# Banded attention: two units at a time, halves of the partitions interleaved on TensorE

## The reference, cut to what matters

```
logits = einsum('bnqhgd,bnkhd->bnhgqk', qb, kw) * (dh ** -0.5)
logits = where(valid, logits, -inf)          # band of 128 keys; block 0 has no block before it
m = maximum(max(logits, axis=-1), sink)
probs = exp(logits - m[..., None])
denom = sum(probs, axis=-1) + exp(sink - m)
out = einsum('bnhgqk,bnkhd->bnhgqd', probs, vw) / denom[..., None]
```

## Time and profile before

| | us |
|---|---|
| median of 3 runs | 4322.08 |
| lowest, highest | 4319.68, 4322.27 |
| profiled execution, its time | 4317.04 |
| its span | 4315.2 |
| TensorE busy | 4166.0 (97%) |
| VectorE busy | 1942.0 (45%) |
| GpSimd busy | 1112.1 (26%) |
| ScalarE busy | 701.1 (16%) |

### The profile page before, as it was taken

The page is one execution under the profiler, slowest core; times in us unless marked ns, Lnnn a source line. Parts: engine busy times, 40 slices in busy tenths (PEclk is TensorE's granted clock), DMA queues, the critical chain, the costliest instruction groups (busy, mean ns, idle before and its releaser), DMA issues.

```text
span 4315.2 us, 43399 instructions
## 1 busy us (share of the span) xinstructions
PE 4166.0 (97%) x17144; PEld 2943.7 (68%) x17144; DVE 1942.0 (45%) x3582; ACT 701.1 (16%) x1452; POOL 1112.1 (26%) x960
## 2 busy tenths in 40 slices
PE   7999999999999999999999999999999989989998
PEld 3448884445588744788833488888886447838887
DVE  3446663246377622433245443333334754454432
ACT  2321110113311100100014310010001321211000
POOL 0003430002344200344300134434442051003443
PEclk9999999998999999999999999999999899989999
DMA  3114443210154442222210122222222132112222
GB/s 119 49 54 168 173 174 135 93 64 30 40 189 175 152 143 88 72 88 86 95 49 20 40 88 88 83 74 88 88 90 66 59 112 59 36 40 78 88 83 73
DMA packets 128105, 387.61 MB, mean 90 GB/s; under 512 B 37984, under 2 KB 41056, under 8 KB 117152
## 3 DMA queue, kind: packets, MB, share of 16 engines
q1 hardware_dynamic: 112592, 302.56, 21.4%
q10 hardware_dynamic: 13824, 75.50, 4.7%
q0 software_dynamic: 1488, 6.78, 0.4%
HBM read 376.40 MB, written 8.39 MB: 89 GB/s over the span
## 4 chain that ended last, share of the span: by engine, by line
PE 93%; DVE 4%; ACT 2%; issue 1%; DMA 0%; POOL 0%; DVEq 0%; ACTq 0%; POOLq 0%
PE bank L762 92%; DVE temporary L2620 1%; PE bank L1202 1%; DVE normed L1911 1%; ACT normed L1449 0%; PE bank L1109 0%; DMA vector_columns<-in_vectors_dram 0%; ACT temporary L1449 0%; ACT area_b L1449 0%; PE bank L1331 0%; DVE area_a L2433 0%; ACT squares L1449 0%; DVE rstd L1926 0%; ACT L1449 0%; DVE temporary L2144 0%
## 5 line engine op out<-in xcount | busy, mean ns | idle before, releaser
L762 PE MATMUL bank<-normed,weight_ring 128*128 128x256 f32 (+2 forms) x3312 | 1025.7, 464 | 17.6 <-DVE normed L1917 5.8
L762 PEld LDWEIGHTS bank<-normed,weight_ring 128*128 128x128 f32 (+1 forms) x3312 | 635.6, 194 | 367.9 <-issue 285.2
L762 PE MATMUL bank<-area_a,weight_ring 128*128 128x512 f32 (+1 forms) x1776 | 636.5, 515 | 8.2 <-issue 8.2
L762 PE MATMUL bank<-area_b,weight_ring 128*128 128x256 f32 (+3 forms) x2000 | 589.2, 441 | 5.9 <-issue 2.8
L762 PEld LDWEIGHTS bank<-area_a,weight_ring 128*128 128x128 f32 x1776 | 339.7, 192 | 282.1 <-issue 259.9
L695 POOL TENSOR_TENSOR area_d<-weight_ring 128x512 f32<-128x512 f32 (+1 forms) x92 | 114.7, 1246 | 1571.0 <-PE bank L762 816.6
L762 PEld LDWEIGHTS bank<-area_b,weight_ring 128*128 128x128 f32 (+2 forms) x2000 | 375.5, 188 | 186.8 <-issue 145.9
L762 PE MATMUL bank<-area_b 128*128 128x256 f32 (+2 forms) x1584 | 345.0, 378 | 16.2 <-ACT area_d L1449 16.2
L762 PEld LDWEIGHTS bank<-area_b 128*128 128x128 f32 (+1 forms) x1584 | 287.1, 194 | 61.0 <-ACT area_d L1449 16.9
L762 PE MATMUL bank<-area_b,area_d 128*128 128x256 f32 x1440 | 326.1, 379 | 0.0
L762 PEld LDWEIGHTS bank<-area_b,area_d 128*128 128x128 f32 x1440 | 273.8, 190 | 37.5 <-issue 0.2
(11 more groups left out here) (296 smaller groups left out, 4788.7 us busy)
## 6 DMA issues: line engine op xcount, KB each, us to landing
weight_ring<-in_weights_dram SPq DMA_DIRECT2D x429, 512.0 KB, 4.6
area_b<-in_weights_dram ACTq DMA_DIRECT2D x48, 1024.0 KB, 4.9
weight_ring<-in_weights_dram SPq DMA_DIRECT2D x35, 1024.0 KB, 4.9
area_b<-in_weights_dram ACTq DMA_DIRECT2D x48, 512.0 KB, 6.3
weight_ring<-in_weights_dram SPq DMA_DIRECT2D x40, 384.0 KB, 4.4
weight_ring<-in_weights_dram SPq DMA_DIRECT2D x24, 256.0 KB, 3.8
low_scratch<-area_d SPq DMA_DIRECT2D x16, 256.0 KB, 2.0
area_d<-low_scratch SPq DMA_DIRECT2D x16, 256.0 KB, 2.7
```

Of the source, the lines that this page charges most:

```text
L762: i = pe.matmul(out, lhsT, rhs, start=start, stop=stop)
```

## The change

Two units that differ only in the half become a pair w (16 pairs). TensorE issues the scores of a pair in the order head 0 half 0, head 0 half 1, head 1 half 0, head 1 half 1, into two products: scores now use banks 0 to 3, and only turned probabilities and outputs use banks 4 to 7, so all eight banks serve the stage. Outputs of a pair are issued key block by key block with the halves alternating, each matmul over both heads at once (256 columns), so there are half as many. The lag is 3 pairs for transposes and 4 for outputs.

VectorE handles the columns of a pair together: the maximum with the sink, the subtraction, the negation, the sum and the reciprocal run once a pair on four columns. ScalarE takes the exponential of the sink once a pair, ahead of the four exponentials, and puts the copies of the turned probabilities in between them. The results are copied out of the banks by VectorE, not ScalarE, four pairs behind. ScalarE now also waits, before it overwrites a turned buffer, for the outputs that read it.

```diff
 stage("at_in", 12 + 4, 2 * 12, 12 * DB + 2 * DB)
-stage("at", 0, 32 * 3, 0)
+stage("at", 32, 32 * 2, 0)
 stage("at_out", DB, 0, DB * DB)
...
         AT_ORDER = {}
-        LAG = 5
-        for u in range(32 + LAG + 1):
-            for what, v in (("scores", u), ("turned", u - LAG), ("output", u - LAG - 1)):
-                if 0 <= v < 32:
-                    AT_ORDER[what, v] = len(AT_ORDER)
+        LAG = 3
+        for w in range(16 + LAG + 1):
+            for what, q in (("turned", w - LAG), ("output", w - LAG - 1)):
+                if 0 <= q < 16:
+                    for half in range(2):
+                        AT_ORDER[what, 2 * q + half] = len(AT_ORDER)
         def at_probs(v):
             return (TM if v % 8 < 4 else D)[:, v % 4, :]
-        def at_column(what, v):
-            o = 16 * ("max", "sum", "sink", "one").index(what) + 2 * (v % 8)
-            return SM[:, o:o + 2]
+        def at_columns(what, w):
+            o = 16 * ("max", "sum", "sink", "one").index(what) + 4 * (w % 4)
+            return SM[:, o:o + 4]
+        def at_scores(v):
+            return AT["at"][0] + v
...
-                po.wait_ge(S("at_one_over"), v + 1)
+                po.wait_ge(S("at_one_over"), v // 2 + 1)
                 for e in range(2):
                     w = at_probs(v)[:, 256 * e + lo:256 * e + 256]
-                    i = po.tensor_scalar(w, w, at_column("one", v)[:, e:e + 1], None, ALU.mult)
+                    i = po.tensor_scalar(w, w, at_columns("one", v // 2)[:, 2 * (v % 2) + e:2 * (v % 2) + e + 1], None, ALU.mult)
                 i.then_inc(S("at_probs"), 1)
...
-            for u in range(32 + LAG + 1):
-                if u < 32:
-                    n, g, half = u // 8, u // 2 % 4, u % 2
-                    rows = slice(64 * half, 64 * half + 64)
-                    s = small()
+            for w in range(16 + LAG + 1):
+                if w < 16:
+                    n, g = w // 4, w % 4
+                    keys = slice((n - 1) * P, (n + 1) * P) if n else slice(0, P)
+                    ms = [product(), product()]
                     for e in range(2):
-                        keys = slice((n - 1) * P, (n + 1) * P) if n else slice(0, P)
-                        mm(sbank(s)[:, 256 * e + (0 if n else 128):256 * e + 256], A[rows, 2 * g + e, n * P:(n + 1) * P],
-                           A[rows, 8 + g, keys], True, True, small_full if e == 1 else None)
-                if 0 <= u - LAG < 32:
-                    v = u - LAG
-                    s = small()
-                    pe.wait_ge(S("at_probs"), v + 1)
-                    for e in range(2):
-                        for b in range(0 if v >= 8 else 1, 2):
-                            i = pe.transpose(sbank(s)[:, (2 * e + b) * P:(2 * e + b + 1) * P],
-                                             at_probs(v)[:, (2 * e + b) * P:(2 * e + b + 1) * P], const("ident"))
-                    i.then_inc(small_full, 1)
-                if u >= LAG + 1:
-                    v = u - LAG - 1
-                    n, g, half = v // 8, v // 2 % 4, v % 2
-                    s = small()
-                    sdone(pe, at_small("turned", v))
-                    for e in range(2):
-                        for b in range(0 if n else 1, 2):
-                            at_tokens = n - 1 + b
-                            mm(sbank(s)[64 * half:64 * half + 64, e * P:(e + 1) * P],
-                               A[:, 12 + at_tokens // 2, at_tokens % 2 * 256 + 64 * g:at_tokens % 2 * 256 + 64 * g + 64],
-                               B[:, 12 + v % 4, (2 * e + b) * P:(2 * e + b + 1) * P], b == (0 if n else 1), b == 1,
-                               small_full if e == 1 and b == 1 else None)
+                        for half in range(2):
+                            rows = slice(64 * half, 64 * half + 64)
+                            mm(pbank(ms[half])[:, 256 * e + (0 if n else 128):256 * e + 256],
+                               A[rows, 2 * g + e, n * P:(n + 1) * P], A[rows, 8 + g, keys], True, True,
+                               product_full if e == 1 else None)
+                if 0 <= w - LAG < 16:
+                    for v in (2 * (w - LAG), 2 * (w - LAG) + 1):
+                        s = small()
+                        pe.wait_ge(S("at_probs"), v + 1)
+                        for e in range(2):
+                            for b in range(0 if v >= 8 else 1, 2):
+                                i = pe.transpose(sbank(s)[:, (2 * e + b) * P:(2 * e + b + 1) * P],
+                                                 at_probs(v)[:, (2 * e + b) * P:(2 * e + b + 1) * P], const("ident"))
+                        i.then_inc(small_full, 1)
+                if w >= LAG + 1:
+                    q = w - LAG - 1
+                    n, g = q // 4, q % 4
+                    ss = [small(), small()]
+                    sdone(pe, at_small("turned", 2 * q))
+                    sdone(pe, at_small("turned", 2 * q + 1))
+                    for b in range(0 if n else 1, 2):
+                        t = n - 1 + b
+                        values = A[:, 12 + t // 2, t % 2 * 256 + 64 * g:t % 2 * 256 + 64 * g + 64]
+                        for half in range(2):
+                            turned = B[:, 12 + (2 * q + half) % 4, :].rearrange("p (e b t) -> p b e t", b=2, t=P)
+                            out = sbank(ss[half])[64 * half:64 * half + 64, 0:256].rearrange("p (e t) -> p e t", t=P)
+                            mm(out, values, turned[:, b], b == (0 if n else 1), b == 1, small_full if b == 1 else None)
...
-            for u in range(32 + LAG):
-                if u < 32:
-                    act.wait_ge(S("at_minus_max"), u + 1)
-                    n, g, half = u // 8, u // 2 % 4, u % 2
-                    for e in range(2):
-                        p = at_probs(u)[:, 256 * e + (0 if n else 128):256 * e + 256]
-                        a(p, p, ACT.Exp, bias=at_column("max", u)[:, e:e + 1],
-                          accum_out=at_column("sum", u)[:, e:e + 1]).then_inc(S("at_exp"), 1)
-                    a(at_column("sink", u), at_column("sink", u), ACT.Exp).then_inc(S("at_exp"), 1)
-                if 0 <= u - LAG + 1 < 32:
-                    v = u - LAG + 1
-                    s = at_small("turned", v)
-                    sfull(act, s)
-                    out, turned = (x.rearrange("p (e k) -> p e k", e=2)[:, :, 0 if v >= 8 else P:]
-                                   for x in (B[:, 12 + v % 4, :], sbank(s)[:, :]))
-                    stook(a(out, turned, ACT.Identity), s)
-                if u >= LAG:
-                    v = u - LAG
-                    n, g, half = v // 8, v // 2 % 4, v % 2
-                    s = at_small("output", v)
-                    sfull(act, s)
-                    rows = slice(64 * half, 64 * half + 64)
-                    stook(a(B[rows, 4 + 2 * g:6 + 2 * g, n * P:(n + 1) * P],
-                            sbank(s)[rows, 0:256].rearrange("p (e t) -> p e t", e=2), ACT.Identity), s)
+            for w in range(16 + LAG - 1):
+                if w < 16:
+                    act.wait_ge(S("at_minus_max"), w + 1)
+                    a(at_columns("sink", w), at_columns("sink", w), ACT.Exp).then_inc(S("at_exp"), 1)
+                for half in range(2):
+                    if w < 16:
+                        for e in range(2):
+                            o = 2 * half + e
+                            p = at_probs(2 * w + half)[:, 256 * e + (0 if w >= 4 else 128):256 * e + 256]
+                            a(p, p, ACT.Exp, bias=at_columns("max", w)[:, o:o + 1],
+                              accum_out=at_columns("sum", w)[:, o:o + 1]).then_inc(S("at_exp"), 1)
+                    if w >= LAG - 1:
+                        v = 2 * (w - LAG + 1) + half
+                        s = at_small("turned", v)
+                        sfull(act, s)
+                        if v >= 4:
+                            sfull(act, at_small("output", v - 4))
+                        out, turned = (x.rearrange("p (e k) -> p e k", e=2)[:, :, 0 if v >= 8 else P:]
+                                       for x in (B[:, 12 + v % 4, :], sbank(s)[:, :]))
+                        stook(a(out, turned, ACT.Identity), s)
...
-            def at_one_over(v):
-                dve.wait_ge(S("at_exp"), 3 * v + 3)
-                own(tt(at_column("sum", v), at_column("sum", v), at_column("sink", v), ALU.add))
-                dve.reciprocal(at_column("one", v), at_column("sum", v)).then_inc(S("at_one_over"), 1)
-
-            for u in range(32 + 1):
-                if u < 32:
-                    n, g, half = u // 8, u // 2 % 4, u % 2
+            def at_one_over(w):
+                dve.wait_ge(S("at_exp"), 5 * w + 5)
+                own(tt(at_columns("sum", w), at_columns("sum", w), at_columns("sink", w), ALU.add))
+                dve.reciprocal(at_columns("one", w), at_columns("sum", w)).then_inc(S("at_one_over"), 1)
+
+            for w in range(16 + LAG + 1):
```

(42 more changed lines are left out.)

## The result

| | before | after |
|---|---|---|
| median, us | 4320.88 (4 runs, 4316.64 to 4322.27) | 4291.14 (4 runs, 4289.52 to 4298.91) |
| ratio | | 0.9938, 95% interval 0.9926 to 0.995 |
| profiled execution: time, span | 4317.04, 4315.2 | 4298.91, 4297.1 |
| TensorE, VectorE, GpSimd, ScalarE busy | 4166.0, 1942.0, 1112.1, 701.1 | 4132.2, 1942.0, 1111.6, 683.7 |

What follows compares the result with a forecast made beforehand. TensorE was taken to bound the loop, then VectorE at 4.45 us a pair; start, pairs and tail put the projection at 1100.9 instead of 1122.37, 21.5 us less: 4300.6 us against the median, range 4295 to 4306 (eight in ten: 4295 to 4313).

Steps and rivals of the forecast that it cites:

- What bounds before: Attention loop before the change: TensorE bounds the full-clock part, 2.67 us a unit, 5.33 for two.
- TensorE, 8 instructions in 0.95 to 1.1 us: Scores and outputs of a pair: instructions of the two halves overlap, so TensorE needs 3.3 us a pair.
- VectorE as the next bound, 4.45 a pair: Pairs with full keys: VectorE work of 2.90 + 0.73 + 0.72 = 4.35 us, plus 0.1 for contention.
- The two result copies: New VectorE work in each pair, copying results out of the banks: 0.36 us each, 0.72 for two.
- The 0.1 for contention: VectorE's small two-input instructions slowed by GpSimd working next to them: 0.1 us more a pair, bound 0.3.
- The exclusive lock: Slower rival: three small VectorE instructions a pair each wait out GpSimd's 0.91 us instruction, 2.7 a pair, 4334 us; chance 0.03.
- The sum: Whole loop: first four pairs 10.2 us, eleven pairs 48.95, tail 11.5; projection starts at 1100.9, 21.5 us less.
- The clock rises before pair 8: Attention loop: granted clock falls to 0.5 after TensorE's first wait, then rises to full before pair 8.
- the smaller spell at half clock: Tail and projection: one spell at half clock, costing 2 to 4 us, counted inside the range.
- The rival that gaps in TensorE's work hold it at 0.50: Attention loop: clock stays at half as TensorE idles 1.1 of 4.45 us; 16 us lost, 4316 us; chance 0.10.
- Waits: Attention loop: only TensorE's wait for the two result banks, freed late in VectorE's iteration, returns.
- All the rest is untouched: what is won here is shifted through: Stages outside the attention loop: unchanged, so the loop's saving passes to the total.

Runs made afterwards that it cites:

- e6: The kernel before with its scores in banks 0 to 3 and nothing else changed: 4316.89 us, ratio 0.9995 to the kernel before.
- e2: The changed kernel with scores and outputs issued half after half, both heads of half 0 first: 4295.81 us, ratio 0.9944 to the kernel before.
- e7: The changed kernel with half 1's scores issued behind half 0's transposes, outputs half after half: 4310.36 us, ratio 0.9976 to the kernel before.
- e3: The changed kernel with both results copied on ScalarE, behind its copies of turned probabilities: 4317.81 us, ratio 0.9999 to the kernel before.
- e4: The changed kernel with half 0's result copied by VectorE, half 1's by ScalarE behind its turned copies: 4325.36 us, ratio 1.0011 to the kernel before.
- e1: The changed kernel run again with no edit: 4289.84 us, ratio 0.9932 to the kernel before.
- e5: The kernel before run again, unchanged: 4317.09 us, ratio 0.9993 to the kernel before.

## Why the prediction was right and wrong

- **What bounds before** (TensorE in the full-clock part): right. e6 frees banks and gains nothing.
- **TensorE, 8 instructions in 0.95 to 1.1 us**: right, 1.07 and 1.01. I read it from the recurrence, whose instructions alternate, and took the alternation for the condition; e2 shows that it isn't.
- **VectorE as the next bound, 4.45 a pair**: right in kind, 4.52 measured. No run leaves out the small instructions once a pair; by the sum, two sets of 0.73 would put VectorE at about 5.25, nearly the 5.33 of before (an estimate). The two result copies were mis-sized: 0.87 from start to start of what follows (1082.12 to 1082.99), not 0.72, since copies of one half take 0.42 each and don't pack like the four of the earlier trace rows. The 0.1 for contention was too much. The source lines of after on VectorE:

```profile
L2254 DVE TENSOR_TENSOR small_columns<-small_columns,vector_columns x16: 161/162/164, 1033.8 to 1094.9; 128x4 f32<-128x4 f32 x16
...
L2255 DVE TENSOR_TENSOR small_columns<-vector_columns,small_columns x16: 161/161/325, 1034.0 to 1095.1; 128x4 f32<-128x4 f32 x16
```

  The longest is 0.325, the median of that line 0.161, with GpSimd busy 38.6 of 49 us next to them. The exclusive lock of the Trainium skill (SBUF — State Buffer, Who interferes with whom), by which such an instruction would wait out one of 0.92 us, isn't in this trace: that rival did not happen.
- **The sum**: first four pairs 10.28 (forecast 10.2), eleven pairs 49.7 (48.95), the loop 21.1 less (21.5). That it comes within 0.4 us is in part luck, since errors cancel: the pairs took 0.8 more than forecast, and the tail behind them some 0.3 less.
- **The clock rises before pair 8**: right; it is at 0.97 from 1046 to 1095, pair 8 begins at about 1060. The tail has the smaller spell at half clock that was in the range (0.86 from 1095 to 1107). The rival that gaps in TensorE's work hold it at 0.50 is wrong here: TensorE idles 0.9 us in every pair at full clock, and it is e7, with TensorE busy 46.9 of 50, that stays at 0.50.
- **Waits**: the one that returned is the one named, TensorE's for the result banks, and VectorE doesn't wait for it. That this needs room in ScalarE's order I had not said; e3 and e4 lose the whole gain on it.
- **The step that failed** is the first paragraph's "All the rest is untouched: what is won here is shifted through". The rest was untouched and still moved: in e1 it gave 2.7 us in the latent attention and 4.6 in the recurrence. The range's lower end was made of the loop's own terms only and had nothing for this; a spell of half clock stood at its upper end alone, as a cost. Of the 9.5 us between the forecast of 4300.6 and 4291.14, another 1.2 is the median of before, 4320.88 and no longer 4322.08. After's own profile gave 2.8 of it behind the attention and lost 5.8 ahead of it; of its runs' median no profile says which stages were short.

What e1's profile accounts for is 27.7 us of its 30.0; the rest is that before's profiled execution was a few us below the median of its runs. What stays open is what places the clock's falls against a stage's start, and why before had the long forms in both of its profiles. Shown is that the long form is a longer time at 1.2 GHz, and that the form goes with when the clock falls after the stage's mark, not what sets it off.

## What to carry to other kernels

Where work with half the array bounds a stage, put the two halves' matmuls next to each other in the queue, in any order: they overlap, and in e7 against after the whole price of keeping them apart fell in the stretch at half clock, which lasted some 50 us instead of 13. When the bound moves to another engine, it is the place of each copy in its engine's order, not the sum of busy times, that decides: the same copy gave pairs of 6.97 us in one place (at a mean clock of 0.76) and 3.98 in another. And in a kernel of some 4300 us give any local saving a range of several us either way for spells of half clock in stages behind it, and compare profiles stage by stage before reading a total.

## What the runs showed of the hardware that was not expected

- Four float32 score instructions of one half take 1.06 us alone, and eight of both halves 1.07, also when all of one half stand ahead of the other's.
- A stage with the same code took 582.1 or 585.3 to 586.8 us, even in two executions of one kernel, through a longer time at 1.2 GHz (granted clock 0.53 against 0.57, 0.67 against 0.80 in e5 against e1); in 14 profiles the short form went with a clock that fell 0.41 us or more after the stage's mark.
- TensorE at 1.2 GHz stayed there for 50 us while busy 94% of the time (e7), and at 2.4 GHz stayed there, but for one spell, while busy 72% (after, 1046 to 1095, granted clock 0.97).
